# Hybrid decoder step on one core: key pages in the place of the stored residual, and state updates on both row halves

## The reference

```
h   = RMSNorm(x) @ W_in            # q, k, v | z, xBC, dt | p
mix = concat[StickBreakingAttn(q, k, v) | Mamba2-SSD(z, xBC, dt) | MultiScalePool(p)]
x   = x + mix @ W_out
x   = x + W_down(silu(causal_dwconv3(RMSNorm(x) W_gate)) * (RMSNorm(x) W_up))
```

```
S_i  <-  decay_i * S_i  +  sum over its 8 tokens of  (weight * x_token) (outer) B_token
```

## Time and profile before

| | us |
|---|---|
| median of 3 runs | 3244.02 (3238.09 to 3248.26) |
| profiled execution | 3247.16 |
| its span | 3245.5 |
| TensorE busy | 3158.5 (97%) |
| VectorE busy | 1898.0 (58%) |
| ScalarE busy | 1346.5 (41%) |
| GpSimd busy | 428.2 (13%) |
| mean DMA rate | 171 GB/s |

### The profile page before, as it was taken

How to read it: one execution, slowest core, us unless ns; L and a number is a source line. 1 busy time by engine, 2 the same in 40 slices (tenths; PEclk the granted TensorE clock), 3 DMA queues, 4 the chain that set the end, 5 groups by cost and what they waited for, 6 DMA issues and landing times.

```text
span 3245.5 us, 62265 instructions
## 1 busy us (share of the span) xinstructions
PE 3158.5 (97%) x23688; PEld 3020.3 (93%) x23688; DVE 1898.0 (58%) x3325; ACT 1346.5 (41%) x1663; POOL 428.2 (13%) x541
## 2 busy tenths in 40 slices
PE   8999998999999999999999999989999999999998
PEld 7999676999999999999999986769999999999998
DVE  5574756466654665466656657555666446644654
ACT  4463666334433333333335546563443333333332
POOL 0000754110000000000300026532100000000002
PEclk9999999999999999999999999999999999999999
DMA  6443799644454445444544448986444444444443
GB/s 201 134 130 108 259 330 332 192 143 155 142 157 143 155 144 156 150 152 135 160 138 130 130 128 276 337 280 189 148 147 155 146 154 146 151 148 152 143 147 107
DMA packets 470007, 554.34 MB, mean 171 GB/s; under 512 B 21279, under 2 KB 415232, under 8 KB 469700
## 3 DMA queue, kind: packets, MB, share of 16 engines
q1 hardware_dynamic: 442339, 467.07, 45.0%
q0 software_dynamic: 27104, 84.75, 7.7%
q10 hardware_dynamic: 385, 0.14, 0.0%
HBM read 535.50 MB, written 16.38 MB: 170 GB/s over the span
## 4 chain that ended last, share of the span: by engine, by line
PE 90%; DVE 2%; DMA 2%; ACT 2%; issue 1%; PEld 1%; DVEq 1%; POOL 0%; SPq 0%; POOLq 0%; ACTq 0%; PEldq 0%
PE ps L1165 26%; PE ps L1167 26%; PE ps L1166 26%; PE ps L1409 3%; PE ps L1421 1%; PE ps L1453 1%; DMA kring<-in_cache_k 1%; PE ps L1561 1%; PE ps L1571 1%; DMA vring<-in_cache_v 1%; PE ps L1498 1%; PE ps L1435 0%; ACT L963 0%; DMA raw<-in_w_out 0%; ACT kT L949 0%
## 5 line engine op out<-in xcount | busy, mean ns | idle before, releaser
L1679 DVE TENSOR_TENSOR wl<-raw,wh 128x1024 fp32r<-128x1024 f32 (+1 forms) x736 | 901.0, 1234 | 989.0 <-ACT wh L782 982.4
L782 ACT ACTIVATE wh<-raw 128x1024 fp32r<-128x1024 f32 (+1 forms) x736 | 764.5, 1041 | 1587.2 <-PE ps L1167 1573.8
L1165 PE MATMUL ps<-fh,wh 128*128 128x320 f32 x2816 | 870.6, 309 | 0.0
L1167 PE MATMUL ps<-fh,wl 128*128 128x320 f32 x2816 | 870.1, 309 | 0.0
L1166 PE MATMUL ps<-fl,wh 128*128 128x320 f32 x2816 | 870.1, 309 | 0.0
L1166 PEld LDWEIGHTS ps<-fl,wh 128*128 128x128 f32 x2816 | 528.6, 188 | 0.2
L1165 PEld LDWEIGHTS ps<-fh,wh 128*128 128x128 f32 x2816 | 528.6, 188 | 0.2
L1167 PEld LDWEIGHTS ps<-fh,wl 128*128 128x128 f32 x2816 | 528.6, 188 | 0.0
L1165 PE MATMUL ps<-ah,wh 128*128 128x320 f32 x1376 | 427.0, 310 | 0.0
L1167 PE MATMUL ps<-ah,wl 128*128 128x320 f32 x1376 | 425.2, 309 | 0.0
L1166 PE MATMUL ps<-al,wh 128*128 128x320 f32 x1328 | 410.3, 309 | 0.0
(11 more groups left out here) (408 smaller groups left out, 3742.0 us busy)
## 6 DMA issues: line engine op xcount, KB each, us to landing
raw<-in_w_gate SPq DMA_DIRECT2D x88, 1024.0 KB, 5.1
raw<-in_w_up SPq DMA_DIRECT2D x88, 1024.0 KB, 5.0
raw<-in_w_in SPq DMA_DIRECT2D x72, 1024.0 KB, 5.2
kring<-in_cache_k SPq DMA_DIRECT2D x256, 256.0 KB, 4.7
vring<-in_cache_v POOLq DMA_DIRECT2D x256, 256.0 KB, 5.0
raw<-in_w_down SPq DMA_DIRECT2D x64, 1024.0 KB, 5.3
raw<-in_w_out SPq DMA_DIRECT2D x32, 1024.0 KB, 7.2
raw<-in_w_down SPq DMA_DIRECT2D x32, 768.0 KB, 4.6
```

The costliest lines, as they stand in the source:

```text
L782: act.activation(wh[:, s % 2, half, :], raw[:, s, half, :], ACT.Copy).then_inc(hi_done, 1)
L1165: pe.matmul(out, wh[:, s % 2, kk, w], hi(row), start=first, stop=False)
L1167: mm = pe.matmul(out, wl[:, s % 2, kk, w], hi(row), start=False, stop=last)
L1679: dve.tensor_tensor(wl[:, s % 2, half, :], raw[:, s, half, :], wh[:, s % 2, half, :].bitcast(F32), ALU.subtract).then_inc(lo_done, 1)
```

## The change

Two parts, which share nothing but the stage. First, 16 KB per partition of the residual (`x_late`, floats 1024 to 5120 of its 5120) are stored to memory (`x_kept`) by Pool at the layer's start, once the norm has read them. Their space becomes the first of two key rings; the second is where the only ring was. Chunk q uses ring q % 2, a page waits for the page two chunks before it, and pages are announced in pairs. SP loads chunk 0 between the loads of the in-projection's last two bodies. After the second piece of the output weights SP loads the residual back, and VectorE waits for that behind the stage's meeting. Second, the operands of the state update get 128 partitions: rows 64 to 127 hold the tokens again, for the upper eight heads and the second group of B. The step `N(i,0)` issues the products of both halves in turn into both banks, `N(i,1)` none; for states 1 to 6 both steps lie one slot later. VectorE makes the second copy (in block 2's `b`, `x` and `cum` steps), and three operations on Pool and ScalarE run on 128 rows.

The changed lines (with the function or branch they are in; indentation cut):

```diff
@@ -106,8 +106,8 @@
-    MIX.update({_s: ("T", _i, 0), _s + 1: ("Y", _i - 1), _s + 2: ("T", _i, 1), _s + 3: ("N", _i - 1, 0),
-        _s + 4: ("N", _i - 1, 1)})
+    MIX.update({_s: ("T", _i, 0), _s + 1: ("Y", _i - 1), _s + 2: ("T", _i, 1), _s + 4: ("N", _i - 1, 0),
+        _s + 5: ("N", _i - 1, 1)})
@@ -151,6 +151,7 @@
+x_at = at[0]
@@ -204,7 +205,9 @@
-kring = sb_at("kring", [P, RING, SBW], F32, raw_at)
+kring = [sb_at("kring0", [P, RING, SBW], F32, x_at + 4096), sb_at("kring1", [P, RING, SBW], F32, raw_at)]
+x_late = x[:].rearrange("p k t -> p (k t)")[:, 1024:1024 + RING * SBW]
+x_kept = nc.dram_tensor("x_kept", (P, RING * SBW), F32, kind="Internal").ap()
@@ -275,7 +278,7 @@
-        bm=at_("bm", [SAMP, 2, NG * NS], r2),
+        bm=at_("bm", [P, 2, NG * NS], r2),
@@ -340,7 +343,8 @@
-k_loaded = [sem(f"k_loaded{i}") for i in range(RING)]
+k_loaded = [[sem(f"k_loaded{i}_{j}") for j in range(RING // 2)] for i in range(2)]
+x_stored, x_back = sem("x_stored"), sem("x_back")
@@ -473,6 +477,17 @@
+        def key_in(q, k):
+            at_page = (q // 4 * 2 + k // 4) * PAGES + 4 * (3 - q % 4) + k % 4
+            page = sync.value_load(pages[0:1, at_page:at_page + 1], min_val=0, max_val=a["cache_k"].shape[1] - 1)
+            sync.dma_start(kring[q % 2][:, k, :], a["cache_k"][l, page].rearrange("s h d -> s (h d)")
+                           ).then_inc(k_loaded[q % 2][k // 2], 16)
+        sync.wait_ge(x_stored, 16 * (l + 1))
+        for k in range(RING):
+            key_in(0, k)
         def state_in(i):
@@ -486,18 +501,14 @@
-        for q in range(CHUNKS):
+        for q in range(1, CHUNKS):
-                slot = RING * (q - 1) + k
-                if q == 0:
+                slot = RING * (q - 2) + k
+                if q == 1:
-                at_page = (q // 4 * 2 + k // 4) * PAGES + 4 * (3 - q % 4) + k % 4
-                page = sync.value_load(pages[0:1, at_page:at_page + 1], min_val=0,
-                                       max_val=a["cache_k"].shape[1] - 1)
-                sync.dma_start(kring[:, k, :], a["cache_k"][l, page].rearrange("s h d -> s (h d)")
-                               ).then_inc(k_loaded[k], 16)
+                key_in(q, k)
@@ -518,6 +529,7 @@
+        sync.dma_start(x_late, x_kept).then_inc(x_back, 16)
@@ -591,6 +603,9 @@
+        pool.wait_ge(h_hi, l * 32 + KT)
+        pool.wait_ge(h_lo, l * 32 + KT)
+        pool.dma_start(x_kept, x_late).then_inc(x_stored, 16)
@@ -640,7 +655,7 @@
         def weighted_x(blk):
-            T = tokens(blk)[1]
+            T = P
@@ -689,8 +704,7 @@
-            pool.tensor_scalar(bm[:, i % 2, :], xtok[0:SAMP, SSW:], con[0:SAMP, K_SEQ + i:K_SEQ + i + 1], None,
-                               ALU.mult).then_inc(s_bm, 1)
+            pool.tensor_scalar(bm[:, i % 2, :], xtok[:, SSW:], tk[:, 5, i:i + 1], None, ALU.mult).then_inc(s_bm, 1)
         def state_out(i):
@@ -1402,11 +1416,11 @@
         def key_page(q, k):
-            pe.wait_ge(k_loaded[k], l * (16 * CHUNKS) + 16 * (q + 1))
+            pe.wait_ge(k_loaded[q % 2][k // 2], l * (16 * CHUNKS) + 32 * (q // 2 + 1))
-                mm = pe.transpose(ps[4 + n % 2][:, j * P:(j + 1) * P], kring[:, k, j * P:(j + 1) * P], ident)
+                mm = pe.transpose(ps[4 + n % 2][:, j * P:(j + 1) * P], kring[q % 2][:, k, j * P:(j + 1) * P], ident)
         def chunk_z(q, bb):
@@ -1468,6 +1482,8 @@
+            if kind == "N" and at[1]:
+                return
@@ -1562,14 +1578,21 @@
             elif kind == "N":
-                i, h = at
-                if h == 0:
-                    pe.wait_ge(s_bm, l * NB + i + 1)
-                    if i == 0:
-                        pe.wait_ge(blk_xw, l * 3 + 3)
+                i = at[0]
+                b1, n1 = USE["N", i, 1]
+                pe.wait_ge(mix_read[b1], l * USES[b1] + n1)
+                pe.wait_ge(s_bm, l * NB + i + 1)
+                if i == 0:
+                    pe.wait_ge(blk_xw, l * 3 + 3)
-                    mm = pe.matmul(bank[:, j * NS:(j + 1) * NS], xw[0:SAMP, (4 * h + j) * P:(4 * h + j + 1) * P],
-                                   bm[:, i % 2, h * NS:(h + 1) * NS], start=True, stop=True)
+                    for h, to in enumerate((b, b1)):
+                        r = slice(SAMP * h, SAMP * h + SAMP)
+                        mm = pe.matmul(ps[MIX_BANKS[to]][:, j * NS:(j + 1) * NS],
+                                       xw[r, (4 * h + j) * P:(4 * h + j + 1) * P],
+                                       bm[r, i % 2, h * NS:(h + 1) * NS], start=True, stop=True)
+                        if j == 3:
+                            mm.then_inc(mix_mm[to], 1)
+                return
             elif kind == "sum":
@@ -2115,12 +2138,20 @@
             elif kind == "b":
+                if blk == 2:
+                    dve.tensor_copy(xtok[SAMP:P, SSW + NS:], bank[0:SAMP, NS:2 * NS])
+                    dve.tensor_copy(tk[SAMP:P, 5, 0:NB], con[0:SAMP, K_SEQ:K_SEQ + NB])
+                    dve.tensor_copy(tk[0:SAMP, 5, 0:NB], con[0:SAMP, K_SEQ:K_SEQ + NB])
             elif kind == "x":
+                if blk == 2 and j == 1:
+                    dve.tensor_tensor(xtok[SAMP:P, 512:SSW].rearrange("p (h d) -> p h d", h=8),
+                                      bank[0:SAMP, :].rearrange("p (h d) -> p h d", h=8),
+                                      tk[0:SAMP, 0, 8:16].unsqueeze(2).broadcast_to([SAMP, 8, DH]), ALU.mult)
@@ -2130,6 +2161,8 @@
+                if blk == 2:
+                    dve.tensor_tensor(tk[SAMP:P, 3, :], bank[0:SAMP, 16:32], tk[0:SAMP, 2, :], ALU.add)
@@ -2265,6 +2298,7 @@
+        dve.wait_ge(x_back, 16 * (l + 1))
         def ffn_low(i, g):
```

## The result

Measured: 3248.52 us median over 20 runs (3237.62 to 3251.32) against 3242.70 us for the kernel before in the same rounds, also 20 runs (3232.78 to 3248.26). The ratio is 1.0017, 95% interval 1.0009 to 1.0024: 5.8 us slower, where 8 us faster was forecast. The profiled execution took 3251.05 us.

A forecast was written before the change was run, and what follows sets the result against it. TensorE and DMA were taken as both nearly full in the sample-state stretch. Terms -12.0 + 0.8 - 2.8 - 1.0 + 4.0 + 2.4 + 0.6 = -8.0 us gave a 3236 us median, own range 3230 to 3242, full range 3224 to 3252.

The forecast's parts named there:

- The return of the residual: Mix stage's tail: 2.1 MB loaded back in SP's queue beside the last value pages, costed at +2.4 us, 1.2 per layer.
- state 7: Mix stage, one of five states (0, 1, 3, 5, 7) whose update was to save its full 1.08 us per layer.
- The rival that named this mechanism: Mix stage's tail: the return starves the last value pages, 15.0 instead of 2.4 us, 3248.6 us in all; chance 0.14.
- The clock: Mix stage: the half-clock dip after a key-page wait would go, taken as -1.0 us, between none and 1.7.
- The updates: Mix stage: 16 alternating records take about the time of 8; -12.0 us for both layers, +0.8 for the longer pair.
- The loss at states 2 and 6: Chunk ends: their updates move behind the wait for attention weights, which returns from 0.54 to 1.62 us, so nothing is saved.
- The key ring and the transfers: Mix stage: pages asked for 16 ahead instead of 8 end key-page waits, -2.8 us; DMA gives back +4.0 us.
- The stretch of the states: Mix stage, 94 us with the sample states: 5 to 6 us shorter if the forecast is right.
- the 358 GB/s of the Trainium skill: One core's HBM share as ceiling for the sample states' transfers: 3.3 us gained per layer there, sum -3.6, 3240.4 us.
- The late state load: Mix stage: a state load first read 0.9 us after landing loses slack as updates shrink; 0.7 us per layer added.
- the store: Layer's start, about 45 to 60 us: the residual's 2 MB store, with DMA busy 0.32 of the time, costs nothing.
- its copies: VectorE's four small extra copies and a 64x512 product in the third block, +0.6 us in all, 0 to 2.8.

The follow-up runs named there:

- late_return: The changed kernel with the residual's return issued after the last value page has landed and behind the third output-weight piece: 3234.78 us, ratio to before 0.9986.
- late_turn: late_return with each update's four lower-half products first, then the four upper, instead of alternating: 3233.12 us, ratio to before 0.9974.
- rows_only: The kernel before plus only the state updates on both row halves, with one key ring and the residual left in place: 3241.34 us, ratio 1.0002.
- late_slots: late_return with the updates of states 2 and 6 back in the last slot of their chunks: 3236.36 us, ratio to before 0.9978.
- late_order: late_return with loads of states 2 and 3 two slots earlier and, per state, both T steps before Y and update: 3232.28 us, ratio to before 0.9974.

## Why the prediction was wrong, point by point

**The return of the residual** is the step that failed. It was costed at +2.4 us "from 0 to 5.8 per layer", since "the new transfer lies some 8 us earlier, where the value ring still has pages in store". Moving it is worth 10 us with the updates and 8 without: the step was mis-sized by a factor of four, inside its upper bound of 11.6 us for both layers. The pages in store were claimed, not read. The row that stood beside the argument belongs to the very last pages; the two pages at the place of the return landed, in the kernel before, 5.4 and 5.8 us after issue and were used at once. The waits for value pages in the same windows as the earlier trace rows, 2.5 us in layer 0, said so and were not used. With 10 in place of 2.4 the sum is -0.4 us, no change, and 5.8 us slower was measured. So the return decided the sign, but some 6 us more were wrong, of which state 7 (below) is 1.7: late_return, which doesn't pay for it, lies 4.5 us below the kernel before (9.4 below to 0.3 above by its interval), where the sum without the return is -10.4.

The rival that named this mechanism, at 0.14, gave 7.5 us per layer, 3248.6 us in all; the measured median is 3248.5. Its mechanism is shown: the pages landed 4.6 and 5.6 us later and TensorE stood 5.7 and 5.2 us longer for value pages. That its total fits so well is partly luck, since the other terms moved too. What stood against it in the prediction, eight value pages in store, did not hold for these two pages.

**The clock.** The sum took 1.0 us off for a dip that would go. Instead the half-clock figure is 10 us above that of the kernel before, 36.8 against 26, and this is clear of its scatter. Not all of it is lost time, as it counts half clock while TensorE stands idle (564 to 568 us above). The late return has 30.5, which the scatter tells apart from neither with safety, so how much of the 10 goes with the return stays open. A second source is in the profiles: the wait of 2.5 us for attention weights behind state 7, new with the updates. In the change half clock follows it in both layers; the wait of 1.62 us before and the 1.93 of late_turn have full clock behind them. First the change, layer 0 and layer 1, then the kernel before and late_turn, layer 0:

```profile
524.70:528.10 3.40, 2.84 (x14) 2.84 (x15) 1.24 (x3) 1.98 (x5) 1.46 (x2) 0.50 1.03 399
2132.40:2139.20 6.80, 6.80 (x51) 4.57 (x49) 0.92 (x2) 2.56 (x6) 1.95 (x4) 0.50 0.90 329
...
532.60:536.00 3.40, 3.35 (x48) 2.98 (x52) 1.42 (x4) 2.63 (x5) 1.46 (x2) 1.00 0.97 344
...
527.80:531.20 3.40, 3.40 (x48) 2.97 (x52) 1.58 (x4) 2.69 (x5) 1.68 (x3) 1.00 1.04 385
```

Over all kernels with this wait of 2.5 us, half clock follows in 8 of 16 places (eight profiles, two layers each); with 1.62 or 1.93 us there, in none of 8. So the wait doesn't bring the fall each time (rows_only has it in both layers at full clock), and what it costs stays open: late_slots and late_order, expected to shorten it, moved only the two waits of 1.18 us behind states 2 and 6, behind which no fall is seen.

**The updates.** The step's size was right to the hundredth (1.09 us, nothing for the longer pair). The loss at states 2 and 6 was right in size: the waits for attention weights behind them rose by about 1.1 us. But the row read for it was another one: 486.72 stands behind state 3, whose wait is 0.53 us after the change as well; behind states 2 and 6 TensorE had not waited at all. State 7 was overlooked: the wait at the end of its chunk grew from 1.62 to 2.47 us. Timeline of the three places (states 2, 6, 7), layer 0, in the kernel before:

```profile
471.08 0.66 PE L1435 MATMUL ps<-con,wq 128*128 128x128 f32 x4
...
517.38 0.66 PE L1435 MATMUL ps<-con,wq 128*128 128x128 f32 x4
...
532.65 0.66 PE L1435 MATMUL ps<-con,wq 128*128 128x128 f32 x4 [1.62 <-ACT wq L963]
```

And in the kernel after:

```profile
466.42 0.66 PE L1449 MATMUL ps<-con,wq 128*128 128x128 f32 x4 [1.18 <-ACT wq L977]
...
510.21 0.66 PE L1449 MATMUL ps<-con,wq 128*128 128x128 f32 x4 [1.18 <-ACT wq L977]
...
525.26 1.11 PE L1449 MATMUL ps<-con,wq 128*128 128x128 f32 x4 [2.47 <-ACT wq L977]
```

With 0.85 us less per layer, the 12.0 us of the sum become 10.3.

**The key ring and the transfers.** The page waits went, as said. The stretch of the states was forecast 5 to 6 us shorter; from one chunk end to another it is 6.1 us shorter in layer 0 (439.34 to 532.65 us before, 438.01 to 525.26 after) and 4.9 in layer 1. 365 and 361 GB/s were reached as means. So the 358 GB/s of the Trainium skill ("DMA: Bandwidth & Descriptors", Specifications) was no ceiling here. The late state load (0.7 us per layer in the sum) was 1.1 us in layer 0 and 4.3 with the late return, by the same code. The sum priced the two parts as terms to be added, while each alone measures as no change and the ring beside the updates as 10 us; that they need each other is how this looks, and only the 10 us are clear of the scatter.

**The other steps** stood as far as the profiles show: the first keys are transposed 0.4 us later in layer 0 than before (314.28 against 313.89 us), so the store costs no more than that. No wait of VectorE for the return is seen, and its copies don't show.

## What to carry to other kernels

A transfer that is free by its size is priced by what lands next to it: list every load of the other queues that is issued within its own landing time, with the slack between landing and use in the kernel before, and put a large transfer that nobody needs soon behind the last load that somebody does. A row for "transfers beside each other" must come from the place in question, not from a similar place later. When two resources are nearly full, a saving on one may be worth little until the other is relieved too, as the updates here without the ring; so cost such edits together, and build each alone.

## What was not expected of the hardware

Two row halves in alternation made the second half of 16 records free (1.09 us against 1.09 for eight); half after half they took 1.61 us. A 2.1 MB load in SyncE's queue made 256 KB loads of GpSimd's queue land in 10.0 and 11.4 us instead of 5.4 and 5.8. Transfers of this kernel reached 365 GB/s over 88 us. The mean granted clock of kernels with the same products lay between 0.9887 (the change) and 0.9927 (late_turn, and the kernel before on one chip), 13 us of half-clock figure on a span of 3240 us, more than most of the edits here are worth; in part this is scatter between runs.
